# Fourier mixing on half the channel frequencies with gathered weight rows, and a reordered expert routing

## The chip, the cores and the metric

The kernel runs on one core of one Trainium2 chip. The metric is the device time of one execution in microseconds (us). Before the change it is 1496.13 us, the median of 3 runs (1495.82 to 1498.43).

The core has five engines, each with its own instruction queue: PE (TensorE, matrix products; PEld is its weight loading), DVE (VectorE), ACT (ScalarE), POOL (GpSimd) and SP (SyncE, which here only starts transfers). They meet through semaphores. A queue is worked off in order, so an instruction that waits holds up everything behind it on its engine.

## The reference

One inference step of a two-layer backbone on 128 prompt tokens and 256 latent tokens, 1024 channels, all in fp32:

```
layer 0: x += g1 * diff_attention(modulate(rmsnorm(x)))   # 8 heads, rotary, cached keys
         x += g2 * swiglu(modulate(rmsnorm(x)))           # 1024 -> 2816 -> 1024
layer 1: x += g1 * fourier_mix(modulate(rmsnorm(x)))
         x += g2 * top2_of_8_experts(modulate(rmsnorm(x)))  # each 1024 -> 2816 -> 1024
y = rmsnorm(x)

def fourier_mix(h, w_f):                      # the 128 prompt and 256 latent tokens apart
    hg = h.reshape(b, l, 4, 256)              # 4 channel groups
    f = jnp.fft.fft2(hg, axes=(1, 3), norm='ortho').real
    return f.reshape(b, l, d) @ w_f           # w_f is 1024 x 1024

def moe_swiglu(h, w_router, w_gu_e, w_down_e):
    probs = softmax(h @ w_router)             # 8 experts
    gates = one_hot weights of the top 2, normalised
    return sum_e gates[e] * swiglu_e(h)
```

The shift, scale and gate vectors of each layer come from a product of the conditioning vector with `ada_w` ("ada" below).

## The kernel before

The 384 tokens are three tiles of 128 (`TILES`; tile 0 is the prompt). Every large product is made three times in a split form: a weight or activation is rounded to a "hi" part, the rest is a "lo" part, and PE adds hi*hi, lo*hi and hi*lo (`mm3`, L1479 to L1481). All weights arrive as units of up to 128x2048 in six slots of `raw`, in one fixed order (`STREAM`, then the expert units `MU`). For each unit ACT writes `ring_hi` (`split_hi`, L689, or `hi`, L865), DVE writes `ring_lo` (`split_lo`, L1002, or `lo`, L1294), and that frees the slot; SP waits for it and starts the load of the unit six places on. The small transforms (ada, Fourier tables, transposes, routing) are plain fp32 products. The order of each engine's work is written out by hand; nothing is scheduled by a program.

The Fourier stage (L1707 to L1737): `turn_normed(2)` transposes the normed rows, ACT and DVE modulate them into `h32` (channels on partitions). First transform: for each token tile and each of 4 channel groups, two products with the table `dft_ch` (256 cosines and 256 sines as one 512-wide operand, L1719); ACT and DVE copy the results to `f_cos` (which is the buffer `xn`) and `f_sin`. Second transform: for each of 8 channel blocks of 128, six products with `dft_p` and `dft_s` over the tokens (L1729 to L1733). ACT rounds each block to `h_hi` (L854), DVE takes `h_lo` (L1280), and `projection(WF0, ...)` multiplies with the four units `wf` of `w_fourier`: unit (n, kh) holds 512 output columns n of 512 weight rows kh. Eight products `ada_unit(5, k)` of the conditioning weights stand among the transforms, since PE has room for them there and their use frees `raw` slots.

The routing stage (L1747 to L1832): logits (L1753, 24 products of 8 columns); DVE finds the top two and writes `mask` and gates; PE counts each token's place within its expert (L1771, L1772); for each expert `select(e)` on DVE (L1345) compares places with 0 to 127, and `number_slots(e)` on PE (L1783, three products of 2 columns) turns that into row numbers. PE also transposes the token rows back (`turn_back`, L1760), ACT copies them to `rows` (L878) and stores them to DRAM; POOL then gathers the rows of expert 0 by an indirect DMA (`bring_rows`, L639). PE spreads the last gates over partitions (`spread_gate`, L1541), transposes the gathered rows (L1793), and the first expert product follows. An expert's gate/up weights come in chunks (`CHUNKS`) of 1024, 1024 and 768 hidden columns, eight units each; `hidden(e, c)` on DVE (L1370, L1373) forms the activations of a chunk. Before the second chunk of expert 0 no other product lies ready, so PE waits there for `hidden(0, 0)`.

Of the kernel before, what the change touches and what calls it, by code (L numbers as in the profile page):

```python
# [23 lines left out]
P = 128  # L24
# [18 lines left out]
RAW = 6  # L43
# [108 lines left out]
def build(nc, t):  # L152

    with ExitStack() as ctx:
# [34 lines left out]
        lam = sb("lam", [P, 1])  # L189
        ssq = sb("ssq", [P, 5, TILES])  # L190
# [65 lines left out]
        def dense(s):  # L256
# [17 lines left out]
            with ExitStack() as q:  # L274
                f_sin = sb("f_sin", [P, TILES, D], F32, q)
            return h32, xn, dft_ch, dft_p, dft_s, v, cos, sin, rope_a, rope_b, ff_hi, ff_lo, tnh, hb, f_sin

        (h32, xn, dft_ch, dft_p, dft_s, v, cos, sin, rope_a, rope_b,
         ff_hi, ff_lo, tnh, hb, f_sin) = over(dense)
# [16 lines left out]
        def rows_or_last(s):  # L296

            with ExitStack() as q:
                pair = (sb("xg", [P, D], F32, q), sb("y_rows", [P, D], F32, q))
            with ExitStack() as q:  # L300
                parts = (sb("y_hi", [P, D], F32R, q), sb("y_lo", [P, D], F32R, q))
            sb("pair_space", [P, 2, D], F32, s)
            return pair + parts
# [10 lines left out]
        def experts(s):  # L314
# [3 lines left out]
                    sb("eh", [P, D], F32, s), sb("eh_hi", [P, 8, P], F32R, s), sb("eh_lo", [P, 8, P], F32R, s),  # L318
# [3 lines left out]
        ((rows, acc), (xg, y_rows, y_hi, y_lo), et, ring_hi_more, ring_lo_more, (xe, (x_tok, x_hT, x_y)),  # L322
         eh, eh_hi, eh_lo, sel, selx, selT) = over(experts)
# [11 lines left out]
        f_cos = xn  # L335
# [9 lines left out]
            sem, ("lane_loaded", "gates_ready", "gvecs_loaded", "xn_last", "cnt_ps", "x_scaled", "cols_ready"))  # L345
        bias_loaded = [sem(f"bias_loaded{g}") for g in range(6)]
# [13 lines left out]
        dft1_ps, dft1_act, dft1_dve, dft2_ps, ft_hi, ft_lo = map(  # L360
            sem, ("dft1_ps", "dft1_act", "dft1_dve", "dft2_ps", "ft_hi", "ft_lo"))
# [26 lines left out]
            "wf": t["w_fourier_1"].rearrange("(k p) n -> p k n", p=P),  # L388
# [31 lines left out]

        GATE_BANKS = (7, 3, 4, 5)
        NORMS = ((0, 0, 0, 1, 16), (1, 1, 2, 0, 24), (3, 0, 3, 1, 32), (4, 1, 5, 0, 40))

        @block.sync
        def _(sp):
            def load(slot, kind, a, b, source=None, loaded=raw_loaded):
# [5 lines left out]
                elif kind == "down":  # L433
                    src = down_source(source[1], a)
                else:
# [8 lines left out]
            def slot_free(before):  # L444

                if STREAM[before][0] == "ada":
                    sp.wait_ge(ada_used, ADA_AT.index(before) + 1)
                else:
                    sp.wait_ge(lo_ready, SPLIT_AT.index(before) + 1)

            for r, src in enumerate((t["c_ctx"], t["c"].rearrange("b n -> (b n)"))):
                sp.dma_start(cvecs[8 * r:8 * r + 8, :], src.rearrange("(k p) -> k p", p=P)).then_inc(cvecs_loaded, 16)
            for u, (kind, a, b) in enumerate(STREAM):
                if u >= RAW:
                    slot_free(u - RAW)
# [1536 lines left out]
```

## Time and profile before

| | |
|---|---|
| time, median of 3 runs | 1496.13 us |
| profiled execution: its own time, its span | 1499.79 us, 1497.9 us |
| mean granted TensorE clock in it | 0.973 of full |
| PE busy | 1419.1 us (95%) |
| DVE, ACT, POOL busy | 1056.2 us (71%), 813.6 us (54%), 200.2 us (13%) |

The profile is of one execution. The span runs from its first instruction to its last; the execution's own time has 1.9 us more around it. "Busy" is the time in which an engine has an instruction in work; for PE that can hide half speed, so the granted clock is read beside it (1.00 is 2.4 GHz, 0.50 is 1.2 GHz). The chain of waits is the sequence of instructions, each released by the one before it, that ended last: only what lies on it can shorten the time. In the timeline a row may stand for a run of equal instructions; the bracket at its end is how long the engine was idle before it, and which instruction ended that. An fp32 product outside `mm3` is two instructions, so a row "x48" is 24 products.

### The profile page before, as it was taken

The page shows a single profiled execution, that of the slowest core. Times are in us where ns is not written, and L with a number is a line of the kernel's source. Part 1 is how long each engine was busy: PE and PEld are TensorE (multiplying, and loading weights), DVE is VectorE, ACT ScalarE, POOL GpSimd, SP SyncE. Part 2 cuts the span into 40 slices and gives each one's busy share as a digit, 9 for nine tenths or more (in the row PEclk, how much of TensorE's full clock was granted, in tenths as well). Part 3 has the DMA queues.
Part 4 walks back from the last instruction along what each step waited for, and adds up shares of the span by engine and source line. Part 5 has one row for each costly group of instructions (what it writes and reads, how often), then busy time and mean ns, then how long its engine had stood idle before and what let it go on. Part 6 is the DMA issues. An engine that isn't in the chain of part 4 may idle for free.

```text
span 1497.9 us, 17389 instructions
## 1 busy us (share of the span) xinstructions
PE 1419.1 (95%) x6951; PEld 1166.2 (78%) x6951; DVE 1056.2 (71%) x997; ACT 813.6 (54%) x806; POOL 200.2 (13%) x320
## 2 busy tenths in 40 slices
PE   5899889999999999998899999999999999999994
PEld 1677547789999994776798898988989889888883
DVE  0642684544555555354789899899998999989994
ACT  2521464432323224243677777777777777777761
POOL 4000373000000000002894000000000000000000
PEclk8999999999999999997999999999999999999996
DMA  9856664734343435415899999999999999999971
GB/s 341 301 192 235 227 242 166 269 126 140 113 141 113 140 125 213 154 34 177 301 337 392 351 406 371 367 411 337 400 373 367 410 340 401 369 366 399 369 286 44
DMA packets 115480, 406.08 MB, mean 271 GB/s; under 512 B 7649, under 2 KB 30354, under 8 KB 97986
## 3 DMA queue, kind: packets, MB, share of 16 engines
q1 hardware_dynamic: 109040, 384.34, 68.3%
q0 software_dynamic: 5280, 17.34, 3.8%
q10 hardware_dynamic: 1074, 3.23, 0.5%
q8 instruction: 57, 0.93, 0.3%
q14 instruction: 29, 0.24, 0.0%
HBM read 394.92 MB, written 9.96 MB: 270 GB/s over the span
## 4 chain that ended last, share of the span: by engine, by line
PE 88%; DVE 6%; DMA 2%; ACT 2%; issue 1%; POOL 0%; DVEq 0%; SPq 0%; ACTq 0%; POOLq 0%
PE ps L1479 25%; PE ps L1481 25%; PE ps L1480 25%; DMA raw<-in_ada_w 2%; PE ps L1493 2%; DVE ring_lo L1294 2%; PE ps L1719 1%; PE ps L1802 1%; PE ps L1541 1%; PE ps L1621 1%; PE ps L1600 1%; PE ps L1520 1%; PE ps L1665 1%; PE ps L1783 1%; PE ps L1732 0%
## 5 line engine op out<-in xcount | busy, mean ns | idle before, releaser
L1294 DVE TENSOR_TENSOR ring_lo<-raw,ring_hi 128x2048 fp32r<-128x2048 f32 (+1 forms) x210 | 452.1, 2168 | 59.3 <-ACT ring_hi L865 57.9
L865 ACT ACTIVATE ring_hi<-raw 128x2048 fp32r<-128x2048 f32 (+1 forms) x210 | 381.8, 1822 | 136.0 <-PE ps L1481 135.6
L1479 PE MATMUL ps<-ring_hi,xe 128*128 128x512 f32 (+1 forms) x576 | 218.5, 379 | 6.6 <-DVE eh L1373 4.0
L1481 PE MATMUL ps<-ring_lo,xe 128*128 128x512 f32 (+1 forms) x576 | 215.6, 374 | 0.0
L1480 PE MATMUL ps<-ring_hi,xe 128*128 128x512 f32 (+1 forms) x576 | 215.0, 373 | 0.0
L1002 DVE TENSOR_TENSOR ring_lo<-raw,ring_hi 128x2048 fp32r<-128x2048 f32 x53 | 120.3, 2288 | 132.4 <-ACT ring_hi L689 132.3
L689 ACT ACTIVATE ring_hi<-raw 128x2048 fp32r<-128x2048 f32 x53 | 101.3, 1914 | 179.9 <-PE ps L1481 145.2
L1294 DVE TENSOR_TENSOR ring_lo_more<-raw,ring_hi_more 128x2048 fp32r<-128x2048 f32 (+1 forms) x70 | 151.8, 2168 | 17.6 <-ACT ring_hi_more L865 17.1
L865 ACT ACTIVATE ring_hi_more<-raw 128x2048 fp32r<-128x2048 f32 (+1 forms) x70 | 127.5, 1821 | 42.6 <-PE ps L1481 42.4
L1479 PEld LDWEIGHTS ps<-ring_hi,xe 128*128 128x128 f32 x576 | 108.9, 189 | 22.7 <-DVE eh L1373 4.5
L1481 PEld LDWEIGHTS ps<-ring_lo,xe 128*128 128x128 f32 x576 | 108.5, 188 | 17.0
L1480 PEld LDWEIGHTS ps<-ring_hi,xe 128*128 128x128 f32 x576 | 108.6, 189 | 15.7
L1479 PE MATMUL ps<-h_hi,ring_hi 128*128 128x384 f32 x336 | 114.7, 341 | 2.5 <-DVE hb L1243 2.5
L1481 PE MATMUL ps<-h_lo,ring_hi 128*128 128x384 f32 x336 | 113.4, 337 | 0.0
L1480 PE MATMUL ps<-h_hi,ring_lo 128*128 128x384 f32 x336 | 113.2, 337 | 0.0
L1479 PE MATMUL ps<-ring_hi,eh_hi 128*128 128x512 f32 x264 | 105.6, 400 | 6.0 <-DVE eh_lo L1358 3.8
L1479 PE MATMUL ps<-ring_hi,h_hi 128*128 128x512 f32 x240 | 99.5, 415 | 5.7 <-DVE h_lo L1066 5.5
L1481 PE MATMUL ps<-ring_lo,eh_hi 128*128 128x512 f32 x264 | 104.4, 395 | 0.0
L1480 PE MATMUL ps<-ring_hi,eh_lo 128*128 128x512 f32 x264 | 104.0, 394 | 0.0
L1481 PE MATMUL ps<-ring_lo,h_hi 128*128 128x512 f32 x240 | 94.6, 394 | 0.0
L1480 PE MATMUL ps<-ring_hi,h_lo 128*128 128x512 f32 x240 | 94.2, 392 | 0.0
L1479 PE MATMUL ps<-ring_hi_more,xe 128*128 128x512 f32 (+1 forms) x192 | 72.6, 378 | 0.2 <-DVE ring_lo_more L1294 0.2
(271 smaller groups left out, 2363.1 us busy)
## 6 DMA issues: line engine op xcount, KB each, us to landing
raw<-in_w_gu_e SPq DMA_DIRECT2D x128, 1024.0 KB, 7.9
raw<-in_w_down_e SPq DMA_DIRECT2D x88, 1024.0 KB, 8.5
raw<-in_ada_w SPq DMA_DIRECT2D x48, 1024.0 KB, 6.6
raw<-in_w_gu_e SPq DMA_DIRECT2D x64, 768.0 KB, 6.7
raw<-in_w_gu SPq DMA_DIRECT2D x44, 512.0 KB, 5.0
raw<-in_w_qkv SPq DMA_DIRECT2D x12, 1024.0 KB, 9.3
raw<-in_w_down SPq DMA_DIRECT2D x11, 1024.0 KB, 7.0
raw<-in_w_o SPq DMA_DIRECT2D x4, 1024.0 KB, 7.8
```

The source lines that it names most:

```text
L689: act.activation(ring_hi[:, s % RING, :], raw[:, u % RAW, :], ACT.Copy).then_inc(hi_ready, 1)
L865: act.activation(ehi[m % RINGM][:, 0:w], raw[:, (MOE_U0 + m) % RAW, 0:w], ACT.Copy).then_inc(hi_ready, 1)
L1002: dve.tensor_tensor(ring_lo[:, s % RING, :], raw[:, u % RAW, :], ring_hi[:, s % RING, :].bitcast(F32), ALU.subtract).then_inc(lo_ready, 1)
L1294: dve.tensor_tensor(elo[m % RINGM][:, 0:w], raw[:, (MOE_U0 + m) % RAW, 0:w], ehi[m % RINGM][:, 0:w].bitcast(F32), ALU.subtract).then_inc(l ...
L1479: pe.matmul(out, l_hi, r_hi, start=first, stop=False)
L1480: pe.matmul(out, l_lo, r_hi, start=False, stop=False)
L1481: return pe.matmul(out, l_hi, r_lo, start=False, stop=last)
L1493: ins = pe.matmul(ps[32 * j:32 * j + 32, 7, :], cond[:, k, :], raw[:, u % RAW, j * HALF:(j + 1) * HALF], start=(k == 0), stop=(k == KC - 1))
L1520: ins = pe.transpose(ps[:, 2 * k + q // 4, (q % 4) * P:(q % 4 + 1) * P], xn[:, k, q * P:(q + 1) * P], ident[:])
L1541: pe.matmul(ps[:, bank, :], ident[:, row:row + 1].to_broadcast([P, P]), gates[:], start=True, stop=True).then_inc(gbc_ps, 1)
L1600: ins = pe.matmul(ps[:, 2 * (i % 2) + m, 0:(P if k == 0 else TOK)], qT[rows, h % 2, k * P:(k + 1) * P], kT[rows, h % 2, keys], start=True, ...
L1621: ins = pe.matmul(ps[:, 5, TOK:HALF], aT[:, i % 2, b * P:(b + 1) * P], vb, start=(b == 0), stop=(b == len(vs) - 1))
```

## The change

Fourier stage. The transform of real channels is symmetric, so only cosines and sines 0 to 127 of each 256-channel group are made (128 + 128 columns rather than 512), and the cosine of number 128 takes the place of sine 0, which is always zero (POOL puts it into the table with a 128x2 copy). The results lie in `waves` (again the buffer `xn`), rotated by 32 partitions per channel group. The second transform makes an "even" part from the cosines and an "odd" part from the sines for each of four groups, and a small product of 32 columns per group (`mid_ps`) for frequency 128. Then even + odd gives frequency k and even - odd gives frequency 256 - k: ACT copies the even part out of PSUM (`tnh`), DVE adds and subtracts into `h32` and copies the one row of frequency 128; ACT and DVE split that. The rows of frequencies 256 - k come in falling order, so the weight rows they meet must stand in that order too: half of each `wf` unit is still loaded by SP (in 3 or 4 pieces instead of one transfer), the other half is gathered by POOL with two indirect DMAs of 128 rows by numbers in `row_idx`, which DVE works out in the qkv stage (`rows_of_waves`). Of the five ada products around the transforms, three stood ahead of the first transform, one behind it and one behind the second; now it is two, two and one. `split_hi` and `split_lo` of the units stand behind the work of the transforms.

Routing. DVE makes one `lo` unit, not three, before it looks at the logits; the other two follow behind the row numbers of expert 0. All six `turn_back` blocks come ahead of the mask products. Only expert 0 is numbered before the first chunk. The selections of experts 1 to 7 (`select`) stand one by one behind the `lo` units of the first chunk, in buffers of their own (`choice`), and `number_others` on PE makes their 21 products and three transposes between the first chunk and the second; `numbers_out` on DVE follows `hidden(0, 0)`.

```diff
@@ POOL, behind norm_pool(2)
+            pool.wait_ge(rows_known, 1)
+            halves_of_rows = t["w_fourier_1"].rearrange("k (h n) -> (k h) n", h=2)
+            for u in range(MOE_U0 - 4, MOE_U0):
+                _, n, kh = STREAM[u]
+                slot_free(pool, u - RAW)
+                for j in range(2):
+                    i = 2 * (2 * kh + j) + n
+                    pool.indirect_dma_start(raw[:, u % RAW, (2 * j + 1) * HALF:(2 * j + 2) * HALF], None, halves_of_rows,
+                                            bass.IndirectOffsetOnAxis(ap=row_idx[:, i:i + 1], axis=0)
+                                            ).then_inc(odd_loaded[u - MOE_U0 + 4], 16)
@@ ACT, Fourier stage
+            for k in range(TILES):
+                act.wait_ge(dft1_ps, 2 * k + 1)
...
+                        ins = act.activation(waves[:, :, k, g, to], part, ACT.Copy)
+                ins.then_inc(dft1_act, 1)
             split_hi(WF0)
+            for g in range(5):
+                if g < 4:
+                    act.wait_ge(dft2_ps, g + 1)
+                    if g >= 2:
+                        act.wait_ge(ft_sum, g - 1)
+                    act.activation(tnh[:, g % 2, :], ps[:, WAVE_BANKS[g], 0:TOK], ACT.Copy).then_inc(ft_even, 1)
+                if g:
+                    act.wait_ge(ft_sum, g)
+                    act.activation(h_hi[:, 2 * g - 2:2 * g, :], h32[:, 2 * g - 2:2 * g, :], ACT.Copy).then_inc(ft_hi, 1)
             split_hi(WF0 + 1)
@@ DVE, Fourier stage
             split_lo(WF0)
+            def low_waves(g):
+                dve.wait_ge(ft_hi, g + 1)
+                both = slice(2 * g, 2 * g + 2)
+                dve.tensor_tensor(h_lo[:, both, :], h32[:, both, :], h_hi[:, both, :].bitcast(F32),
+                                  ALU.subtract).then_inc(ft_lo, 1)
+
+            for g in range(4):
+                even, odd = tnh[:, g % 2, :], ps[:, WAVE_BANKS[g] + 1, 0:TOK]
+                dve.wait_ge(ft_even, g + 1)
+                dve.scalar_tensor_tensor(h32[:, 2 * g, :], odd, first_k[:, g:g + 1], even, ALU.mult, ALU.add)
+                link(dve.tensor_tensor(h32[:, 2 * g + 1, :], even, odd, ALU.subtract))
+                dve.wait_ge(mid_ps, 1)
+                quarter = slice(32 * g, 32 * g + 1)
+                dve.tensor_copy(h32[quarter, 2 * g + 1, :], ps[quarter, 6, 0:TOK]).then_inc(ft_sum, 1)
+                if g:
+                    low_waves(g - 1)
+            low_waves(3)
+            ada_rows_out(5)
             split_lo(WF0 + 1)
@@ DVE, routing and the first chunk
-            for m in range(RING):
-                lo(m)
...
+            lo(0)
             dve.wait_ge(logit_ps, 1)
...
+            lo(1)
             dve.wait_ge(cnt_ps, 1)
             dve.tensor_copy(cnt[:], ps[:, 6, 96:96 + N_EXP]).then_inc(cnt_ready, 1)
+            lo(2)
...
+                        if (e, c) == (0, 0):
+                            numbers_out()
...
+                if m + 1 < N_EXP:
+                    select(m + 1)
@@ PE, Fourier stage
+            for k in range(TILES):
+                pe.wait_ge(h32_ready, 6 + k + 1)
+                pe.wait_ge(h32_upper, 6 + k + 1)
+                for g in range(4):
...
+            for k in range(5, 7):
+                ada_unit(5, k)
+            pe.wait_ge(dft1_act, TILES)
+            pe.wait_ge(dft1_dve, TILES)
...
+            for g in range(4):
+                if g == 3:
+                    pe.wait_ge(ft_sum, 1)
...
                 ins.then_inc(dft2_ps, 1)
             ada_unit(5, 7)
-            pe.wait_ge(ft_lo, KC)
...
+                if (s, k) == (0, 2):
+                    pe.wait_ge(ft_lo, 4)
+
+            pe.wait_ge(ft_sum, 3)
+            pe.wait_ge(ft_lo, 2)
             projection(WF0, 1, None, 0, turn_and_spread)
@@ PE, routing
+            for j in range(4):
                 spread_gate(3, j, GATE_BANKS[j])
...
             turn_gathered(0, 0)
...
+            def number_others():
+                pe.wait_ge(cnt_ready, 1)
+                for e in range(1, N_EXP):
+                    number_slots(e)
...
+                    if n == 0 and (e, c) == (0, 1):
+                        number_others()
```

What stands in PE's row of instructions in the Fourier stage before, from the ada products behind the transposes (`raw,cond`) to the second of the eight blocks of the second transform:

```order
L1493 MATMUL ps<-raw,cond 32x512 x12
L1719 MATMUL ps<-dft_ch,h 128x512 x24
L1493 MATMUL ps<-raw,cond 32x512 x4
L1729 MATMUL ps<-dft_p,xn 128x128
L1730 MATMUL ps<-dft_p,f_sin 128x128
L1732 MATMUL ps<-dft_s,xn 128x256
L1733 MATMUL ps<-dft_s,f_sin 128x256
L1732 MATMUL ps<-dft_s,xn 128x256
L1733 MATMUL ps<-dft_s,f_sin 128x256
```

And the same stretch now, to the second of eight half blocks (`32x...` are the small products for frequency 128):

```order
L1591 MATMUL ps<-raw,cond 32x512 x8
L1816 MATMUL ps<-dft_ch,h 128x256 x24
L1591 MATMUL ps<-raw,cond 32x512 x8
L1828 MATMUL ps<-dft_p,xn 32x128 x4
L1828 MATMUL ps<-dft_s,xn 32x256 x8
L1836 MATMUL ps<-dft_p,xn 128x128
L1838 MATMUL ps<-dft_s,xn 128x256 x2
```

The first transform has the same 24 products of half the width; a block of the second has three products where it had six, and there are still eight blocks; one ada product moved from ahead of the first transform to behind it.

PE's routing before, from the logits (`wr`) to the first expert product (`xe`):

```order
L1753 MATMUL ps<-wr,h 128x8 x24
L1760 MATMUL ps<-ident,h 128x128 x16
L1772 MATMUL ps<-mask,tri 128x8
...
L1760 MATMUL ps<-ident,h 128x128 x8
L1541 MATMUL ps<-gates,ident 128x512
L1783 MATMUL ps<-vals,sel 128x2 x3
L1818 MATMUL ps<-mask,ones 128x8 x3
L1783 MATMUL ps<-vals,sel 128x2 x18
L1783 MATMUL ps<-vals,selx 128x2 x3
L1541 MATMUL ps<-gates,ident 128x512 x3
L1827 MATMUL ps<-ident,selx 128x128 x3
L1793 MATMUL ps<-ident,xg 128x128 x8
```

PE's routing now:

```order
L1861 MATMUL ps<-wr,h 128x8 x24
L1868 MATMUL ps<-ident,h 128x128 x24
L1880 MATMUL ps<-mask,tri 128x8
...
L1886 MATMUL ps<-vals,sel 128x2 x3
L1921 MATMUL ps<-mask,ones 128x8 x3
L1639 MATMUL ps<-gates,ident 128x512 x4
L1896 MATMUL ps<-ident,xg 128x128 x8
```

And PE between the last product of the first chunk of expert 0 (`ring_lo_more,xe`) and the first of its second chunk:

```order
L1579 MATMUL ps<-ring_lo_more,xe 128x512
L1886 MATMUL ps<-vals,sel 128x2 x3
L1886 MATMUL ps<-vals,sel_y 128x2 x6
L1886 MATMUL ps<-vals,sel_h 128x2 x9
L1886 MATMUL ps<-vals,selx 128x2 x3
L1935 MATMUL ps<-ident,selx 128x128 x3
L1577 MATMUL ps<-ring_hi,xe 128x512
```

The 21 numbering products and the three transposes of `selx` left the routing and stand at the border of the chunks.

## Rows read from the trace of the kernel before

**Rows 1.** The page: shares of the span in the chain that ended last, by engine.

```profile
PE 88%; DVE 6%; DMA 2%; ACT 2%; issue 1%; POOL 0%; DVEq 0%; SPq 0%; ACTq 0%; POOLq 0%
```

**Rows 2.** Waits of ACT (700 to 1480) and PE (735 to 1480): total, times, longest us.

```profile
ACT ring_hi L865 <- PE ps L1481: 135.6, 163, 5.9
...
PE ps L1479 <- DVE ring_lo L1294: 2.8, 4, 1.3
```

**Rows 3.** Chain of waits, Fourier stage: start us, length us, engine, tile, line, instructions.

```profile
579.05 2.71 PE ps L1493 x24
581.76 20.80 PE ps L1719 x48
...
622.32 0.50 PE ps L1479
```

**Rows 4.** PE timeline, second transform: start us, us, engine, line, instructions.

```profile
603.81 0.39 PE L1730 MATMUL ps<-dft_p,f_sin 128*128 128x128 f32 x2
604.03 0.60 PE L1732 MATMUL ps<-dft_s,xn 128*128 128x256 f32 x2
604.47 0.59 PE L1733 MATMUL ps<-dft_s,f_sin 128*128 128x256 f32 x2
```

**Rows 5.** Timelines of DVE and ACT: one row of the qkv stage, then Fourier.

```profile
110.07 2.29 DVE L1002 TENSOR_TENSOR ring_lo<-raw,ring_hi 128x2048 fp32r<-128x2048 f32 x1 [3.17 <-ACT ring_hi L689]
...
584.02 1.91 ACT L689 ACTIVATE ring_hi<-raw 128x2048 fp32r<-128x2048 f32 x1 [2.89 <-DMA raw<-in_w_fourier]
605.96 0.49 ACT L854 ACTIVATE h_hi<-ps 128x384 fp32r<-128x384 f32 x1 [4.42 <-PE ps L1733]
...
607.67 0.55 DVE L1280 TENSOR_TENSOR h_lo<-ps,h_hi 128x384 fp32r<-128x384 f32 x1
```

**Rows 6.** Indirect DMAs: POOL before them, issue (ns min/median/max), landing (us), scatter's landing.

```profile
575.96 0.55 POOL L579 TENSOR_TENSOR rstd<-msq,mhalf 128x1 f32<-128x1 f32 x1
...
L639 POOL DMA_INDIRECT xg<-rows_dram,pick_to x8: 951/1022/1365, 689.1 to 1250.5; - x8
...
DMA to landing us min/median/max: 4.2/7.8/9.4
...
acc_dram<-y_rows,send_to POOLq DMA_INDIRECT x7, 12.2
```

**Rows 7.** Chain of waits, routing stage.

```profile
673.64 2.29 DVE ring_lo L1294
...
679.98 0.60 PE ps L1772 x2
...
682.71 1.80 PE ps L1760 x8
...
687.53 7.88 PE ps L1783 x42
695.41 4.58 PE ps L1541 x6
...
703.11 0.47 PE ps L1479
```

**Rows 8.** Timelines of PE, ACT and POOL: end of logits, gather, chunk border.

```profile
672.16 3.41 PE L1760 MATMUL ps<-ident,h 128*128 128x128 f32 x16
...
684.55 1.02 ACT L878 ACTIVATE rows<-ps 128x1024 f32<-128x1024 f32 x1 [4.42 <-PE ps L1760]
...
689.08 1.36 POOL L639 DMA_INDIRECT xg<-rows_dram,pick_to  x1 [26.00 <-DMA rows_dram<-rows]
...
700.14 1.04 PE L1793 MATMUL ps<-ident,xg 128*128 128x128 f32 x8
...
729.44 0.52 PE L1479 MATMUL ps<-ring_hi,xe 128*128 128x512 f32 x1 [4.03 <-DVE eh L1373]
```

**Rows 9.** Stretches: length; busy us (instructions) of PE, PEld, DVE, ACT, POOL; clock; DMA.

```profile
687.00:688.00 1.00, 1.00 (x11) 1.00 (x10) 0.11 (x1) 0.00 (x0) 0.00 (x0) 1.00 0.69 283
689.00:694.00 5.00, 5.00 (x25) 5.00 (x25) 2.14 (x4) 0.00 (x0) 1.36 (x1) 0.50 0.33 105
```

More of the change, by code:

```diff
@@ L434, in load @@
                     src = down_source(source[1], a)
+                elif kind == "wf":
+                    for first, row, n, j in wave_pieces(b):
+                        sp.dma_start(dst[first:first + n, j, :],
+                                     t["w_fourier_1"][row:row + n, a * HALF:(a + 1) * HALF]).then_inc(loaded[slot], 16)
+                    return
                 else:
@@ L868, in _ @@
             modulate(3, 4, None)
-            for m in range(RING):
+            for m in range(RING - 1):
                 hi(m)
@@ L1722, in _ @@
[L1722 to L1734 removed]
+            pe.wait_ge(dft_ready, 1)
@@ new lines, in _ @@
+            for k in range(TILES):
+                pe.wait_ge(h32_ready, 6 + k + 1)
+                pe.wait_ge(h32_upper, 6 + k + 1)
+                for g in range(4):
+                    out = ps[:, 2 * k + g // 2, (g % 2) * 256:(g % 2 + 1) * 256].rearrange("p (u n) -> p u n", u=2)
+                    for q in range(2):
+                        ins = pe.matmul(out, h32[:, 2 * g + q, k * P:(k + 1) * P],
+                                        dft_ch[:, q, :].rearrange("p (u n) -> p u n", u=2)[:, :, 0:P],
+                                        start=(q == 0), stop=(q == 1))
+                    if g % 2:
+                        ins.then_inc(dft1_ps, 1)
@@ new lines, in _ @@
+            for k in range(5, 7):
+                ada_unit(5, k)
+            pe.wait_ge(dft1_act, TILES)
+            pe.wait_ge(dft1_dve, TILES)
+            for k in range(TILES):
+                for g in range(4):
+                    table, cols = (dft_p[:, 0, :], slice(0, P)) if k == 0 else (dft_s[:, k - 1, 0, :], slice(P, TOK))
+                    ins = pe.matmul(ps[32 * g:32 * g + 32, 6, cols], waves[:, 1, k, g, 32 * g:32 * g + 32], table,
+                                    start=(k < 2), stop=(k != 1))
@@ new lines, in _ @@
+            ins.then_inc(mid_ps, 1)
+            for g in range(4):
+                if g == 3:
+                    pe.wait_ge(ft_sum, 1)
+                for u in range(2):
+                    bank = WAVE_BANKS[g] + u
+                    pe.matmul(ps[:, bank, 0:P], waves[:, u, 0, g, :], dft_p[:, u, :], start=True, stop=True)
+                    for k in range(2):
+                        ins = pe.matmul(ps[:, bank, P:TOK], waves[:, u, 1 + k, g, :], dft_s[:, k, u, :],
+                                        start=(k == 0), stop=(k == 1))
@@ L1762, in turn_back @@
                 ins.then_inc(tokT_ps, 1)
-            for n in range(4):
+            for n in range(2 * TILES):
                 turn_back(n)
@@ L1773, in _ @@
             ins.then_inc(pos_ps, 1)
-            for n in range(4, 2 * TILES):
-                turn_back(n)
-            spread_gate(3, 0, GATE_BANKS[0])
             def number_slots(e):
```

197 lines of the change are left out of this document (102 added, 95 removed).

## The prediction

> **What bounds the kernel now.** I read the shares of the chain of waits first: PE holds 88% of it [rows 1], so the time is mostly what PE has to do, and the question is which products and waits of PE go and which come. Then the waits: over the expert phase ACT waited 135.6 us for PE, in 163 cases, and PE for DVE's `ring_lo` only 2.8 us [rows 2]. The stream of weights is ahead of PE there, so whatever starts the expert phase earlier ends the kernel earlier by as much. Then the two stages that the change touches. In the Fourier stage PE runs without a gap from 581.76 to the first projection product at 622.32 [rows 3]: 40.6 us in which everything else only follows. In the routing stage the chain goes from engine to engine: DVE's third `ring_lo` ends at 675.93, ACT's exponentials, PE's mask products at 679.98, eight transposes, 42 instructions that number slots (7.88 us), gates (4.58 us), and the first expert product at 703.11 [rows 7]. Last the border of the first two chunks: PE idles 4.03 us there until 729.44 [rows 8].
>
> **Fourier stage, PE.** An ada product is 2.71 / 3 = 0.90 us, a product of 512 columns of the first transform 20.80 / 24 = 0.87 us [rows 3]. In the second transform one of 128 columns takes 0.22 us and one of 256 takes 0.44 us from start to start [rows 4], so width sets the price. Now: two ada products, 579.05 to 580.85. The tiles are modulated by then one after another, before it, so the loop by tile doesn't wait. 24 products of 256 columns, 10.4 us: to 591.25. Two ada products: 593.05. The 12 products of 32 columns: 4 x 0.22 + 8 x 0.44 = 4.4 us if they stand one behind the other, 1.1 us if four strips run side by side, as an ada product does (four strips of 512 columns in 0.90 us, where one full product takes 0.87). The ada row is the nearest; I take 1.5. Then eight half blocks of 0.22 + 2 x 0.44 = 1.1 us, 8.8 us, and an ada product: PE is through at 604.25.
>
> The projection also waits for the third sum and the second `low_waves`. The third pair of half blocks ends at 593.05 + 1.5 + 6.6 = 601.15. Behind it come ACT's copy of 384 columns (0.49, as L854), three DVE instructions of 384 columns (0.55 each, as L1280 [rows 5]; the one-row copy streams as many columns) and a subtraction of 768, about 1.0 by the same row, with gaps of 0.1: about 604.6. So the start moves from 622.32 to 604.6: **17.7 us less**. With 1.1 for the small products it is 18.2; with 4.4 everything behind them is 2.9 later: 14.8. Of the ends I take the one near 1.5 for the reason given.
>
> What lies beside that: ACT and DVE copy 9 and 12 pieces where they copied 12 and 12; the last tile's follow PE by about 1 us, behind two ada products. `split_hi(WF0)` needs the gathered half. POOL is free at 576.5 and its two indirect DMAs for the first unit take about 1.0 us each to issue and 4.2 to 9.4 us to land [rows 6]: at most 588, and ACT comes to it at 590.5, when the last tile's copies are done. Before, the same instruction waited for the weights at 584.02 [rows 5]. The second and third unit follow by 2 us each and are wanted from 608 on; the fourth waits for an ada product at 592. SP's 14 pieces instead of 4 transfers carry half the bytes, and the expert units behind them are not wanted before the first chunk. So the loads cost nothing. What stands behind that wait on ACT are the four even copies, on which DVE's sums and then PE wait: without the cover each us of lateness beyond 592 is a us of the sum. PE's new wait for the first sum, ahead of the fourth group, is over by then: first group 596.8, copy and three DVE instructions by 599.3, and the third group ends at 601.15. `rows_of_waves` in the qkv stage is 21 DVE instructions, none wider than 128 columns, an estimate of 0.2 us each from 0.55 for 384; DVE idles 3.17 us ahead of one `ring_lo` there [rows 5] and ran ahead of PE, so nothing, at most 0.5 (nor can it gain, since it only adds).
>
> **Routing.** The logits end at 672.16 [rows 8] (times of before; the shift of 17.7 comes off at the end). With two `lo` of 2.29 us gone from ahead of them, DVE looks at the logits at once, not at 675.93. From there to the mask products it took 679.98 - 675.93 = 4.05 us [rows 7]: now 676.3. PE first does all six transposes: 3.41 us and 1.80 us (at the slow clock) more [rows 7, 8]: 676.5 to 677.4. The gather left at 689.08, 4.53 us after the last row copy began at 684.55 [rows 8]; that copy now begins at 677, so the gather leaves at 681.5. Mask products, selection and numbering of expert 0 (about 4 us behind 676.5) are done by then. It lands 4.2 to 7.8 us later [rows 6]; I take 6, since two expert units are loaded beside it: 687.5. PE meanwhile makes four gates of 4.58 / 3 = 1.5 us and is through at about the same time. From its transposes to the first product 703.11 - 700.14 = 2.97 us [rows 7, 8]: 690.5 where it was 703.11, 12.6 us less; 10.8 to 14.4 with the ends of the landing.
>
> The clock: after the 4.03 us without work at the chunk border, PE's products come at half speed for a while; numbering too, in 689 to 694, stands at 0.50, 1.2 GHz, after running at 1.00 before [rows 9]. Now PE has little to do between 677 and 690, so the first expert products may fall to 1.2 GHz for some 4 us, which costs 2; I take 1: **11.6 us less** (8.8 to 14.4).
>
> **The border.** The 42 numbering instructions come at 11 per us at 2.4 GHz and 25 in 5 us at 1.2 GHz [rows 9]: 3.8 to 8.4 us, with the three transposes 4.3 to 8.9. They replace the wait of 4.03 us, which hides that much. I take 5.5, as most of them follow a stretch at full clock: **1.5 us more** (0.3 to 4.9). The slow products behind the border stood there before as well. The seven selections cost DVE 0.56 each beside `lo` (0.55 for 384 columns [rows 5]): 2.85 us per unit, against 96 products from 703.11 to 725.41, 2.79 us per unit, on PE; it loses 0.5 us in eight units and starts three units ahead. Behind `numbers_out` on DVE and the copy of `selT` on ACT, which now wait for the end of the numbering, stand `lo` and `hi` of the twelfth unit; PE wants that three units, 8.4 us, later. Nothing.
>
> **Sum.** 17.7 + 11.6 - 1.5 = 27.8 us. The profiled execution took 1499.79 us, 1.9 more than its span: it becomes 1472.0. It was 3.7 us above the median, so the median becomes **1468.3 us**. The ends: 18.2 + 14.4 - 0.3 = 32.3, 1463.8 us; 14.8 + 8.8 - 4.9 = 18.7, 1477.4 us.
>
> **Rivals.** (1) The reordered routing gives most of its gain back: the gather takes 7.8 us, the first chunk starts at 1.2 GHz and the numbering at the border runs at that clock, while the Fourier part is as forecast. 17.7 + 8.8 - 4.9 = 21.6: 1474.5 us. For it speaks that every stretch of small products in this stage fell to 0.50; against it, that each fell only after some us at 1.00.
>
> (2) The gathers run one after another, each starting when the one before has landed. No row shows two in flight, since `xg` is one buffer. Eight of 7.8 us end at 576.5 + 62.4 = 638.9; with hi and lo, 1.91 + 2.29, the last unit is ready at 643.1. PE wants it three units of 36 products (0.232 us each by the 2.79 above) and the gates after 604.6, at about 632: 11 us late, 1479.4 us. At the 12.2 us of the indirect DMAs that add into DRAM [rows 6] it is ready at 678.3, 46 us late, and the kernel takes 1514.6 us, **slower than before**; from 9.9 us per gather on, the 27.8 are gone. Against it: a gather's issue ends in 1.0 us and POOL goes on. The Trainium skill (DMA: Bandwidth & Descriptors, section SWDGE vs HWDGE vs iDMA) says that one queue is allocated to transfers that GpSimd describes. Read as strict order, it gives 1479.4 us; nothing in this trace shows two such transfers together, so it stands as a rival only.
>
> (3) The change doesn't do what it says in one point: the table is read in two pieces of 128 columns, and should that cost as much as 512, the first transform stays at 20.8 us: 10.4 of the gain are gone, 1478.7 us. The widths in rows 4 speak against it.
>
> (4) All goes well: 1464 us.
>
> **How the numbers follow.** Forecast, 1465 to 1473 us: 0.58. Rival 1, 1473 to 1478: 0.22. Rival 4: 0.07. Rival 3: 0.04. Rival 2 at 7.8 us: 0.04; at 9.9 us and more: 0.05. The range 1463 to 1478 us takes in both ends of the unknown prices and leaves out rivals 2 and 3. Slower by over 0.2% (3 us, what a measurement can tell from no change) is rival 2 at its dear end, 0.05; for within 0.2% nothing speaks but its edge, 0.01; faster 0.94.
>
> **What would show it.** The first transform in 10.4 us; 12 strip products in 1.1 to 2 us; the first projection product 23.8 us behind the start of the first transform (40.6 before); ACT's first `ring_hi` of `w_fourier` not waiting for a DMA; between the last logit and the first expert product 18.3 us instead of 31; 24 numbering and transposing products at the border in 5 to 6 us. It would be wrong if ACT or PE waited for `in_w_fourier`, or if PE waited for the third sum for more than 1 us.

## The result: 13.5 us faster, where 27.8 were forecast

The changed kernel takes 1483.68 us, the median of four runs (1480.66 to 1485.17), where the kernel before took 1497.22 beside it (1495.82 to 1498.43). The ratio is 0.9903, with a 95% interval of 0.989 to 0.9917. The forecast of 1468.3 us and its range, 1463 to 1478, are both missed: 13.5 us came of 27.8. The two profiled executions are further apart, 1499.79 and 1480.66 us (spans 1497.9 and 1478.8), since the one of before was 2.6 us above its median and the one of after 3.0 below; the working below goes by these spans, 19.1 us.

The chain of waits of the changed kernel: start us, length us, engine, tile, line, instructions. It answers to [rows 3] and [rows 7].

```profile
580.59 10.56 PE ps L1816 x48
591.15 1.85 PE ps L1591 x16
593.00 1.08 PE ps L1828 x24
...
602.97 1.00 PE ps L1591 x8
603.97 0.66 issue
604.63 0.47 PE ps L1577
...
655.33 5.21 PE ps L1868 x24
...
665.00 8.48 DMA xg<-rows_dram,pick_to
673.52 1.10 PE ps L1896 x8
674.62 1.62 issue
676.24 0.47 PE ps L1577
698.76 5.66 PE ps L1886 x42
704.42 0.74 PE ps L1935 x3
705.16 0.43 PE ps L1577
```

Before the change the logits ended at 672.31 (PE's row of them: start, length):

```profile
665.06 7.25 PE L1753 MATMUL ps<-wr,h 128*128 128x8 f32 x48
```

Read it from stage to stage. The projection starts at 604.63 where it started at 622.32: 17.69 us gained, what the Fourier part was to bring. From there to the end of the logits (655.33) it takes 50.7 us, before 50.0: 0.7 lost, though nothing was changed there (e1 below, with its tiles at the old places, has 49.8). From the end of the logits to the first expert product it takes 20.9 us, before 30.8: 9.9 gained. From the first expert product to the end of the span it takes 802.6 us (676.24 to 1478.8), before 794.8 (703.11 to 1497.9): **7.8 us lost**. That is where the gain went: 17.7 - 0.7 + 9.9 - 7.8 = 19.1.

The border of the first two chunks explains 2 of the 7.8: 6.2 us pass between them where it was 4.2, of which PE was idle for 4.03 [rows 8]. From the first product of the second chunk to the end of the span it is 774.0 us, before 768.4: 5.6 more. That rest is no wait. PE waits in the expert phase for the same things and as long as before. This is its list, total, times, longest, first before (from 735 us on, beside [rows 2]) and then now (from 708 us on):

```profile
PE ps L1479 <- DVE eh_lo L1358: 3.8, 1, 3.8
PE ps L1811 <- DVE y_lo L1407: 2.4, 1, 2.4
```

```profile
PE ps L1577 <- DVE eh_lo L1450: 3.8, 1, 3.8
PE ps L1577 <- DVE ring_lo L1392: 2.7, 4, 1.3
PE ps L1914 <- DVE y_lo L1503: 2.4, 1, 2.4
```

What differs is the single product. The groups of PE by line with forms kept apart: line, out<-in, shapes, count, then busy us and mean ns of one. First the kernel before:

```profile
L1481 PE MATMUL ps<-ring_lo,eh_hi 128*128 128x512 f32 x264 | 104.4, 395 | 0.0
L1480 PE MATMUL ps<-ring_hi,eh_lo 128*128 128x512 f32 x264 | 104.0, 394 | 0.0
L1479 PE MATMUL ps<-ring_hi,ff_hi 128*128 128x512 f32 x132 | 51.7, 392 | 0.0
L1480 PE MATMUL ps<-ring_hi_more,eh_lo 128*128 128x512 f32 x88 | 34.3, 390 | 0.0
```

And the changed kernel:

```profile
L1579 PE MATMUL ps<-ring_lo,eh_hi 128*128 128x512 f32 x264 | 105.0, 398 | 0.0
L1578 PE MATMUL ps<-ring_hi,eh_lo 128*128 128x512 f32 x264 | 105.0, 398 | 0.0
L1577 PE MATMUL ps<-ring_hi,ff_hi 128*128 128x512 f32 x132 | 52.6, 399 | 0.0
L1578 PE MATMUL ps<-ring_hi_more,eh_lo 128*128 128x512 f32 x88 | 34.5, 392 | 0.0
```

The mean holds some 0.16 us in which a product still runs while the next has begun; from start to start, ring products with `eh_lo` are 227.6 ns apart before and 233.4 after (steps under 300 ns). By their means the groups of ring products have become 2 to 7 ns longer, some thousand times over, in the feed-forward layer (`ff_hi`) as well, long before the Fourier stage. One group keeps its mean, the first of each three with `eh_hi` (400 ns in both); from start to start it went from 231.5 to 233.4.

### The profile page after: what moved, and what is told of

Read it like the earlier page. It is cut to its first block, busy times and chain, and to the rows that moved or that the text cites. A ratio compares the mean times of both kernels' runs of the same rounds, so it can differ in the third digit from the quotient of the medians.

```text
span 1478.8 us, 17392 instructions
## 1 busy us (share of the span) xinstructions
PE 1405.7 (95%) x6927; PEld 1154.5 (78%) x6927; DVE 1062.3 (72%) x1026; ACT 813.4 (55%) x803; POOL 220.7 (15%) x329
## 4 chain that ended last, share of the span: by engine, by line
PE 89%; DVE 5%; DMA 3%; ACT 1%; issue 1%; POOL 0%; DVEq 0%; SPq 0%; ACTq 0%; POOLq 0%
PE ps L1577 26%; PE ps L1579 26%; PE ps L1578 26%; PE ps L1591 2%; PE ps L1905 1%; DMA raw<-in_w_qkv 1%; DVE ring_lo L1392 1%; PE ps L1698 1%; PE ps L1719 1%; DMA raw<-in_ada_w 1%; PE ps L1816 1%; PE ps L1639 1%; PE ps L1763 1%; DMA xg<-rows_dram,pick_to 1%; PE ps L1861 0%
## 5 line engine op out<-in xcount | busy, mean ns | idle before, releaser
L1392 DVE TENSOR_TENSOR ring_lo_more<-raw,ring_hi_more 128x2048 fp32r<-128x2048 f32 (+1 forms) x70 | 151.8, 2168 | 20.1 <-ACT ring_hi_more L922 19.7
```

Source lines behind the costliest of these rows:

```text
L1392: dve.tensor_tensor(elo[m % RINGM][:, 0:w], raw[:, (MOE_U0 + m) % RAW, 0:w], ehi[m % RINGM][:, 0:w].bitcast(F32), ALU.subtract).then_inc(l ...
```

## The experiments

**Theory P**: these places make the products slower. **Theory R**: the places don't matter; it is the execution, or the changed instructions. For the routing, where 9.9 us were gained and 11.6 expected, **theory G**: the gather is late because its issue on GpSimd runs beside VectorE's subtractions (2.43 us, 1.36 in [rows 8]). Theory W came later, from the runs. Every ratio is to runs of the kernel before on the same chip; times of different chips are compared by these ratios.

**e1, the small tiles at the end of memory.**

```diff
-        w_row = sb("w_row", [P, 4])
-        row_idx = sb("row_idx", [P, 8], I32)
-        first_k = sb("first_k", [P, 4])
...
+        def fourier_small(s):
+            sb("skip_all", [P, 19200], F32, s)
+            return sb("w_row", [P, 4], F32, s), sb("row_idx", [P, 8], I32, s), sb("first_k", [P, 4], F32, s)
+
+        w_row, row_idx, first_k = over(fourier_small)
```

> The changed kernel, with its three new small tiles (w_row, row_idx, first_k) put at the end of the memory, so that every other tile has the address that it has in the kernel before; nothing else differs. Theory P (the 96 bytes by which the new tiles push all later tiles make the expert products slower: ring products 233.3 ns apart instead of 228.8): the pitch is back at 228 to 229.5 ns, the time from the first expert product to the end falls from 802.6 us to 796 to 797, the profile's span to about 1472 (1471 to 1474). Theory R (the pitch is a property of the execution or of the changed instructions, not of the places): pitch near 233, span 1478 to 1483 as in the changed kernel. The first expert product stands near 676.2 us in both.

Measured: 1471.32 us (1469.61 to 1474.64) against 1498.92, ratio 0.9816 (0.98 to 0.9832). The products are back:

```profile
L1581 PE MATMUL ps<-ring_hi,eh_lo 128*128 128x512 f32 x264 | 104.1, 394 | 0.0
L1580 PE MATMUL ps<-ring_hi,ff_hi 128*128 128x512 f32 x132 | 51.7, 392 | 0.0
```

The gain is 27.6 us, where the prediction's sum was 27.8. Theory P holds, R falls. (The stretch from the first expert product is 798.6 us, not the 796 to 797 expected: the first chunk took 23.4 us from the start of its first product to that of its last, 21.9 in the kernel before, and the granted clock at 674 to 676 us, in its first products, was 0.50.)

**e2, the kernel before with 96 bytes more.**

```diff
+        sb("pad", [P, 24])
         ssq = sb("ssq", [P, 5, TILES])
```

> The kernel before, with an unused tile of 96 bytes where the change puts its three small tiles; all instructions are the same. Theory P: ring products go from 228.8 to about 233.3 ns apart, those of the extra ring slot from 231 to 228, the stretch from the first expert product (703.1 us) to the end grows by 6 to 7.5 us to about 801.5, and the time rises to 1502 to 1506 us. Theory R: 1495.8 to 1498.4, as it was, and the pitch stays.

Measured: 1509.2 us against 1498.92, ratio 1.006 (1.0044 to 1.0077). An unused tile alone costs 10 us. That is more than expected, as the price was reckoned for the expert phase only (800.1 us, 5.3 more). The first transform already begins 2.9 us later, since the layers before it make the same products (with `h_lo` 400 ns, 392 in the kernel before), and 2.0 more pass between projection and logits.

```profile
L1481 PE MATMUL ps<-ring_hi,eh_lo 128*128 128x512 f32 x264 | 104.9, 397 | 0.0
```

**e4, the Fourier half alone, no tile moved.** The edit is the change without the hunks on routing (`choice`, `select`, `numbers_out`, `number_others`, `turn_back`, and the order of `hi` and `lo` there).

> The Fourier half of the change alone on the kernel before (routing as before), the small tiles at the end of memory so that no other tile moves. By the prediction's first term the projection starts 17.7 us earlier (604.6 instead of 622.3), and the time falls by 17 to 18 us to 1479 to 1480 if theory P holds, since then nothing is lost later. If something else in the Fourier half slows the expert products (theory R), the gain is only 10 to 12 us, and the time 1485 to 1487.

Measured: 1479.98 us against 1498.92, ratio 0.9881 (0.9863 to 0.9899): 18.9 us less by the medians, where 17 to 18 were expected. The routing half is then worth 8.7 us, the step from here to e1.

**e8, the changed kernel again.**

> The changed kernel unaltered, on the chip of the others. Theory P: its ring products have again 398 to 399 ns with ff_hi and eh_lo, and it is 10 to 13 us slower than e1_old_places against the same runs of the kernel before (ratio 0.989 to 0.992). Rival: the earlier profile was an odd execution; ratio near 0.982 and 392 to 394 ns.

Measured: 1485.03 us against 1498.38, ratio 0.9906 (0.9891 to 0.9921), products of 398 and 399 ns as before. Against e1 the moved tiles cost 0.009 of 1498 us, some 13 us.

**e5, all later tiles moved by 64 bytes instead of 96.** Rule A was my guess at what counts: whether the two operands stand alike within 64 bytes.

```diff
+        sb("pad", [P, 16])
         ssq = sb("ssq", [P, 5, TILES])
```

> As e1_old_places (small tiles at the end), with an unused tile of 64 bytes where the change had put them: all later tiles move by 64 bytes instead of 96. The ring stays at a multiple of 128; h_hi, ff_hi, xe and eh_hi go from 64 past such a multiple to 0 past it (in the changed kernel they stand at 32). Rule A (a product is slower when the ring slot that it reads and its other operand stand differently within 64 bytes): nothing is lost, ring products with ff_hi and eh_lo keep 392 and 394 ns (392 and 394 in e1_old_places, 399 and 398 in the changed kernel), time as e1_old_places, 0.9800 to 0.9835 of the kernel before. Rule B (any move away from the old places costs, or the distance within 128 bytes counts): 397 to 400 ns, 0.988 to 0.992.

Measured: 1463.96 us against 1498.38, ratio 0.9775 (0.976 to 0.979). Neither rule: it is faster than at the old places.

```profile
L1582 PE MATMUL ps<-ring_hi,eh_lo 128*128 128x512 f32 x264 | 103.6, 392 | 0.0
L1583 PE MATMUL ps<-ring_lo,eh_hi 128*128 128x512 f32 x264 | 103.6, 392 | 0.0
L1581 PE MATMUL ps<-ring_hi,ff_hi 128*128 128x512 f32 x132 | 51.8, 392 | 0.0
```

Now ring and operands all begin at multiples of 128. So what counts would be the difference within 128 bytes (rule D), or beginning there (rule E).

**e6, ring and operands 32 bytes further on**, 32 and 96 past a multiple of 128: their difference is 64, as before the change.

```diff
+        sb("pad", [P, 8])
         ring_hi = sb("ring_hi", [P, RING, UNIT], F32R)
```

> As e1_old_places, with an unused tile of 32 bytes ahead of ring_hi: the ring and all that follows move by 32 bytes together, so that both operands of a ring product stand at 32 within 64 bytes. Rule A (only a difference between the two counts): ring products with ff_hi and eh_lo keep 392 to 394 ns, and the time is that of e1_old_places, 0.9800 to 0.9835 of the kernel before. Rule C (an operand that doesn't begin at a multiple of 64 bytes costs, whatever the other does): 397 to 400 ns or more, ratio 0.988 to 0.993.

Measured: ratio 0.9822 (0.9807 to 0.9837), the same as e1, with 394 and 392 ns. Rule C falls: no operand begins at a multiple of 64, and nothing is lost.

**e10, both 32 past a multiple of 128**: difference 0 again. The edit is e5's and e6's together.

> As e5_moved_64, with the ring and every later tile 32 bytes further on: ring and other operands all stand 32 past a multiple of 128, so their difference is 0 again. Rule D (the difference of the two operands' places within 128 bytes counts: 0 is best, 64 between, 32 or 96 worst): time as e5_moved_64, ratio 0.976 to 0.979, ring products with eh_hi, eh_lo near 394 and 392 ns. Rule E (the tiles must begin at a multiple of 128, or of 64, themselves): ratio 0.981 or more, 398 to 400 ns.

Measured: ratio 0.9776 (0.9748 to 0.9804), as e5, not as e1. The interval is wide and overlaps that of e1; the products decide, above all the group of `eh_hi`, which has 400 ns in e1:

```profile
L1582 PE MATMUL ps<-ring_hi,eh_hi 128*128 128x512 f32 x264 | 104.1, 394 | 6.0 <-DVE eh_lo L1455 3.8 <-DVE ring_lo L1397 2.2
L1583 PE MATMUL ps<-ring_hi,eh_lo 128*128 128x512 f32 x264 | 103.8, 393 | 0.0
L1584 PE MATMUL ps<-ring_lo,eh_hi 128*128 128x512 f32 x264 | 103.6, 393 | 0.0
L1582 PE MATMUL ps<-ring_hi,ff_hi 128*128 128x512 f32 x132 | 51.7, 392 | 0.0
```

**e12, the kernel before with 64 bytes more.**

```diff
+        sb("pad", [P, 16])
         ssq = sb("ssq", [P, 5, TILES])
```

> The kernel before with an unused tile of 64 bytes where the change puts its small tiles, and nothing else. Rule D: its tiles now stand as the ring does (difference 0), so it gains what e5_moved_64 gained over e1_old_places, 6 to 8 us: ratio 0.9945 to 0.9965. Rival (the gain of e5 came with the changed instructions): ratio 0.999 to 1.001.

Measured: 1489.55 us against 1498.04, ratio 0.9946 (0.9931 to 0.9961). An unused tile of 64 bytes gains 8.5 us and one of 96 loses 10, with not one instruction changed. The difference of rule D sorts all fourteen profiles. From the first expert product to the end of the span, us (with the new routing, the numbering at the border is in it):

| difference within 128 bytes | routing as before | new routing |
|---|---|---|
| 0 | e12 788.5 | e5 790.1, e9 791.6, e10 792.1, e11 788.4 |
| 64 | before 794.8, e4 794.6 | e1 798.6, e3 795.5, e6 798.8, e7 795.9 |
| 32 | e2 800.1 | changed 802.6, e8 802.4 |

From the first product of the second chunk on, where routing and numbering are over, the groups are 761.6 to 763.9, 768.2 to 769.1 and 773.6 to 774.0 us. No kernel has a difference of 96.

One group doesn't fit the rule as worded, for two operands of one product. The fourth slot of the ring (`ring_hi_more`) lies among the later tiles and moves with them, so that it and `eh_hi` differ by 0 in every kernel; yet its products with `eh_hi` take 394 ns before, 392 in the changed kernel and 389 in e12. So what is shown is a rule on the distance between the ring and the tiles behind it. That a product's own two operands make it is argued.

**e3, the subtractions taken from beside the gather.** The second goes into the wait ahead of the positions, the third behind `xe`; places as in e1.

```diff
             link(dve.memset(posm[:, :, N_EXP:], -1.0))
+            lo(1)
...
-            lo(1)
             dve.wait_ge(cnt_ps, 1)
             dve.tensor_copy(cnt[:], ps[:, 6, 96:96 + N_EXP]).then_inc(cnt_ready, 1)
-            lo(2)
             for half in range(2):
                 low_xe(0, half, half)
+            lo(2)
```

> As e1_old_places, with two of VectorE's low-part subtractions moved: the second from behind pick_to into the wait ahead of the positions, the third behind the two parts of xe, so that none runs while GpSimd issues the first gather of rows. Theory G (the gather's issue took 2.43 us since a subtraction ran beside it): the issue takes 0.9 to 1.4 us, the first expert product comes 1.0 to 1.5 us earlier than in e1_old_places, and the time is 1 to 1.5 us lower. Rival: the issue was long since its engine was cold or the queue was busy; then it stays at 2.2 to 2.5 us, and the two kernels are within 0.5 us.

Measured: 1471.28 us, ratio 0.9809 (0.9794 to 0.9824): no gain that can be told from e1. The issue did fall, from 2.12 to 1.06 us:

```profile
664.87 1.06 POOL L691 DMA_INDIRECT xg<-rows_dram,pick_to  x1 [20.39 <-DVE pick_to L1476]
```

The rows landed 4.53 us behind its start, 8.12 in e1. But they weren't what ended last. The moved subtraction, 659.71 to 662.00, held up the positions, and PE's products of the gates behind them, in this execution at a granted clock of 0.50, ended 3 us behind the landing at 669.40:

```profile
665.95 6.63 PE L1642 MATMUL ps<-gates,ident 128*128 128x512 f32 x8
672.41 1.04 PE L1899 MATMUL ps<-ident,xg 128*128 128x128 f32 x8
```

From the first look at the logits to the first expert product it took 19.9 us, 20.1 in e1. So e3 decides nothing about theory G.

**e7, both subtractions behind `xe`**, nothing put ahead of the positions.

```diff
-            lo(1)
             dve.wait_ge(cnt_ps, 1)
             dve.tensor_copy(cnt[:], ps[:, 6, 96:96 + N_EXP]).then_inc(cnt_ready, 1)
-            lo(2)
             for half in range(2):
                 low_xe(0, half, half)
+            lo(1)
+            lo(2)
```

> As e1_old_places, with VectorE's second and third low-part subtraction both moved behind the two parts of xe; nothing runs on VectorE beside the issue of the first gather, and nothing is put ahead of the positions. Theory G: the issue takes 0.9 to 1.2 us (2.1 to 2.4 with a subtraction beside it), from pick_to to the first expert product it is 10.6 to 10.9 us instead of 12.0, and from the end of the logits 18.8 to 19.2 instead of 20.2; the time falls 1.0 to 1.4 us below e1_old_places, to about 1470. Rival: the gates' products on TensorE, 5.5 to 6.6 us, end as late as the rows land, and the subtractions are then late for the second and third unit; no gain, or up to 1 us lost.

Measured: 1467.06 us, ratio 0.979 (0.9777 to 0.9804). From the first look at the logits to the first expert product 16.2 us, 4 less than e1, where theory G had 1.3 to give; the rows landed after 4.24 us. So the issue's length is not the main thing. What else do the subtractions do there? Each frees a slot of `raw`, on which SyncE starts the next load of 1 MB. Hence **theory W**: the gather shares the DMA engines with two loads that the early subtractions set off.

**e11, the subtractions where the change has them, the loads held.** On e5:

```diff
                     sp.wait_ge(lo_ready, MOE0 + m - RAW + 1)
+                if m == RAW + 1:
+                    sp.wait_ge(xg_loaded, 16)
```

> As e5_moved_64 (the subtractions stand right behind pick_to, as in the changed kernel), with one wait added on SyncE: the load of weight unit 7, which the second subtraction releases, waits until the first gathered rows have landed, and those behind it with it. Theory W (the rows land late because the subtractions release two 1 MB weight loads that share the DMA engines with the gather: 383 to 415 GB/s and a DMA share of 1.0 at 669 to 673.5 us in the changed kernel): the rows land 3 to 4 us behind the issue's end instead of 6, from the end of the logits to the first expert product 17.5 to 18.5 us instead of 20.0 to 20.9, and the time falls 1.5 to 2.5 us below e5_moved_64, though the issue beside a subtraction still takes 1.5 to 2.4 us. Theory G alone (only the issue's length counts): as e5_moved_64, within 0.5 us. A third way: the held loads come late for the units at 690 to 700 us, and the time rises.

Measured: 1462.88 us against 1498.04, ratio 0.9751 (0.9734 to 0.9769; e5 0.9775). First the changed kernel: SyncE's loads, then stretches (length; busy us and instructions of PE, PEld, DVE, ACT, POOL; granted clock, DMA share, GB/s).

```profile
666.53 2.81 SPq L504 DMA_DIRECT2D raw<-in_w_gu_e  x2
```

```profile
667.00:669.00 2.00, 2.00 (x3) 0.67 (x2) 1.77 (x1) 0.60 (x1) 0.43 (x1) 0.50 0.54 102
669.00:671.00 2.00, 2.00 (x4) 0.85 (x3) 0.00 (x0) 0.60 (x1) 0.00 (x0) 0.50 0.99 383
671.00:673.00 2.00, 1.09 (x3) 0.16 (x1) 0.00 (x0) 1.19 (x2) 0.00 (x0) 0.92 1.02 418
```

Then e11: the gather in its chain of waits, SyncE's next loads, and the stretch in which the rows move.

```profile
665.71 4.48 DMA xg<-rows_dram,pick_to
```

```profile
670.28 6.43 SPq L510 DMA_DIRECT2D raw<-in_w_gu_e  x3
```

```profile
666.00:668.00 2.00, 2.00 (x4) 0.75 (x3) 2.00 (x3) 1.11 (x2) 1.10 (x1) 0.50 0.14 29
668.00:670.00 2.00, 2.00 (x4) 0.57 (x2) 0.44 (x1) 0.60 (x1) 0.00 (x0) 0.66 0.67 234
```

With the loads held the rows take 4.48 us from issue to landing, 7.12 in e5, from which e11 differs by that wait alone, and 8.48 in the changed kernel. Theory W holds, and the loads cost 2.6 us of landing. (What counts is that they start just behind the issue: in e3 one load, set off 2.9 us ahead of it, was still running, and the rows took 4.53.) From the first look at the logits to the first expert product it is 16.4 us (17.5 to 18.5 expected), 20.0 in e5, 20.9 in the changed kernel; 0.9 of the 3.6 to e5 is that the issue itself came earlier, 9.2 us behind the first look and not 10.1. The ratio is 0.0024 lower than that of e5, some 3.6 us, with intervals that overlap.

Theory G isn't excluded by this. The issue took 1.39 us here and 1.06 in e9, which comes to 16.4 us too, but no run has an issue of over 2 us with the loads held. Beside the loads the rows landed after 7.1 us where the issue took 1.4 to 1.5 (e5, e10), 8.0 to 8.1 where it took 2.1 (e1, e6) and 8.5 where it took 2.4 (changed, e8). So about 1 us of the 8.48 may be the issue's; that share is argued.

**e9, both mends**: e5's places and e7's order.

> Both mends together: the tiles placed as in e5_moved_64 (small tiles at the end, all later tiles at multiples of 128 bytes like the ring) and the two low-part subtractions behind xe as in e7_lo_behind. If the two are independent, the gains add: ratio 0.9775 (e5) and 0.979 against 0.9816 (e7 against e1) make 0.975, that is 1460 to 1462 us where the kernel before takes 1498. Rival: e5's lower time already holds part of e7's gain; ratio 0.977.

Measured: 1461.39 us (1457.91 to 1464.39), ratio 0.9754 (0.974 to 0.9767), as expected. With e11 it is the fastest: 36.6 us below the kernel before, where the change as made gave 13.5.

## Why the prediction was wrong

**The step that failed** is in its first paragraph: "whatever starts the expert phase earlier ends the kernel earlier by as much". That takes the phase itself for unchanged, and it was not: 7.8 us longer, 5.6 of them behind the border in the products themselves (e2, where nothing but the places changed, has 5.1 there). The sum had no term for it, because the diff was read instruction by instruction, and the hunk that declares three tiles holds none. The layers ahead of the Fourier stage lost by it too, 2.9 us in e2. By the medians the places cost 13.5 us (e8 against e1), about what the forecast is off; with the tiles out of the way the change gives 27.6 us.

That 27.6 is so near the sum of 27.8 is partly luck. In e1's profile the projection comes 18.6 us earlier (17.7 in the sum), the routing gives 10.6 (11.6) and the expert phase with its border takes 3.9 more (1.5): 25.5 us of span, with 0.2 from the stretch between.

**Fourier part: right.** First transform 10.56 us (10.4), strips 1.08 us (1.5, so they run side by side), first projection product at 604.63 (604.6), 24.1 us behind the start of the first transform (23.8). That the start of the projection is right to the digit is luck: the first transform begins at 580.5 here, and at 576.7 to 579.7 in e1, e3, e4 and e7, whose large tiles lie as before. The 24.1 us are the same in all of them, to 0.02. (PE's 40.6 us before weren't quite without a gap: ACT and DVE held the last 1.1 of them, 621.18 to 622.32. The term doesn't hang on that.) ACT's first `ring_hi` of `w_fourier` follows its copies without waiting for a DMA, where it waited 2.89 us [rows 5]:

```profile
589.46 0.72 ACT L899 ACTIVATE xn<-ps 128x256 f32<-128x256 f32 x3 [2.73 <-PE ps L1816]
590.05 1.92 ACT L738 ACTIVATE ring_hi<-raw 128x2048 fp32r<-128x2048 f32 x1
```

**Rival 2, gathers one after another: excluded.** Six of the eight are issued 0.30 us behind the end of the one before, some 1.25 us from start to start, and they land 5.8 to 8.1 us behind their issue, so several are in flight:

```profile
579.21 1.00 POOL L677 DMA_INDIRECT raw<-in_w_fourier,row_idx  x1 [0.30 <-issue]
580.51 0.95 POOL L677 DMA_INDIRECT raw<-in_w_fourier,row_idx  x1 [0.30 <-issue]
581.76 0.95 POOL L677 DMA_INDIRECT raw<-in_w_fourier,row_idx  x1 [0.30 <-issue]
...
DMA to landing us min/median/max: 5.8/7.5/8.1
```

The Trainium skill (DMA: Bandwidth & Descriptors, section SWDGE vs HWDGE vs iDMA), read as strict order, was the reason for that rival; with eight of them here, the trace speaks against this reading.

**Routing: the landing was mis-sized.** 20.9 us from logits to first expert product, not 18.3. The gather left 9.7 us behind the logits (9.3 forecast); it took 8.48 us, where the term had 6 and its range ended at 7.8, the median of [rows 6], whose longest is 9.4; the tail was 2.7 (2.97). I had seen that loads run beside it, but not that the change itself sets them off: two `lo` now end just as the gather starts. The half speed that I put at 1 us for the first expert products did not come here; in e1, e6 and e10 it came, and the first chunk took 23.2 to 23.4 us, 22.1 here.

**The border: 2.0 us, 1.5 forecast.** 42 numbering instructions and three transposes, 5.66 + 0.74 us, in place of 4.2.

**Rival 1** gave 1474.5 us for other reasons than those that held; a slower expert phase stood in no rival.

## What to carry to other kernels

A diff that declares a tile moves every tile behind it: compare the places of the big matmul operands before and after, and treat their distance within 128 bytes as part of the change. Here an unused tile cost 10 us of 1498 or gained 8.5, as much as a rewritten stage. And where a step is moved forward, follow what it releases: a subtraction that ends early starts a 1 MB load, and the small gather that all wait for takes nearly twice as long to land.

## What the runs showed of the hardware

**Places in memory and TensorE.** Ring products with `eh_lo`, 512 columns, take 392 to 393 ns where the two operands begin at the same place within 128 bytes, 394 at a distance of 64, 397 to 398 at 32. Products with `ff_hi` take 392, 392 and 398 to 399. No other compute engine is needed for it: the ring products beside which ACT, DVE and POOL all stood still, 219 to 250 in a profile, are 227.5 ns apart in e12, 229.1 in the kernel before and 233.2 in e2. Which reads get in each other's way, the streamed ring with the loading of the other operand or something else, no run here separates, and the fourth slot speaks against a rule of two operands alone; nor whether distances beyond 128 bytes count. The Trainium skill (SBUF — State Buffer, section SBUF: two separate sides) has it that on the engines' side only the port pair shared by VectorE and GpSimd causes contention, and that TensorE never waits on anyone. That rule is on engines against each other; e2 and e12, with the same instructions on all engines, show that a product's length still hangs on where its operands lie.

**An indirect DMA's issue beside VectorE.** 1.06 us in e3, e7 and e9 without a subtraction beside it, 2.12 in e1 and 2.43 in the changed kernel with one. It ends about 0.9 us behind the subtraction that runs when it starts: that one ended 1.50 us into the issue in the changed kernel, 1.19 in e1, 0.59 in e5 and 0.45 in e11, and the issue took 2.43, 2.12, 1.52 and 1.39, 0.93 to 0.94 more each time. A subtraction that begins during an issue doesn't lengthen it: one that began 0.24 us into it left it at 1.09 (802.14 us, kernel before). The same section says that a VectorE instruction with two inputs from memory can lock GpSimd out for its whole length, if GpSimd's own instruction reads that memory; the subtraction has two, the gather reads its row numbers there, and these numbers agree.

**The same 65 instructions, 9.2 or 13.8 us.** The last stretch ahead of the routing in e7 and then e9, columns as above:

```profile
643.00:653.20 10.20, 9.21 (x65) 9.21 (x66) 7.12 (x20) 8.72 (x15) 0.72 (x2) 0.79 0.01 3
```

```profile
640.00:654.60 14.60, 13.75 (x65) 13.75 (x66) 7.08 (x19) 8.79 (x15) 0.58 (x2) 0.50 0.20 67
```

The granted clock was 0.79 on average in the one, part at 2.4 and part at 1.2 GHz, and 0.50, all at 1.2 GHz, in the other; PE had been busy for 8.36 and 8.21 of the 10 us ahead. One such stretch moves a span by 4.5 us, which is why stages were compared here from one event to the next, and kernels by several runs.
